# Gate and up products moved into the output projection's program, with their first two weight tiles loaded and split there

## The reference

```python
def finish_layer(x, o_n, o_f, g_n, g_f, w_o, g_post_mix, g_pre_ffn, g_post_ffn, w_gate, w_up, w_down):
    mixed = jnp.concatenate([rms_norm(o_n, g_n), rms_norm(o_f, g_f)], axis=-1) @ w_o
    x = x + rms_norm(mixed, g_post_mix)
    hf = rms_norm(x, g_pre_ffn)
    ffn = (jax.nn.silu(hf @ w_gate) * (hf @ w_up)) @ w_down
    return x + rms_norm(ffn, g_post_ffn)
```

## Time and profile before

| what | value |
|---|---|
| median of 3 runs | 1980.43 us (1977.78 to 1982.19) |
| the profiled execution | 1979.99 us, of it 1978.3 us span from first to last instruction |
| TensorE busy with matmuls | 1806.4 us, 91% of the span |
| VectorE, ScalarE, GpSimd busy | 917.3, 600.1, 266.2 us (46%, 30%, 13%) |
| mean granted clock of TensorE | 0.954 of full |
| gate and up products, three lines | 341.9 + 339.5 + 339.2 us busy, matmuls overlapping |

### The profile page before, as it was taken

How to read it: one execution, slowest core, us unless ns; L and a number is a source line. 1 busy time by engine, 2 the same in 40 slices (tenths; PEclk the granted TensorE clock), 3 DMA queues, 4 the chain that set the end, 5 groups by cost and what they waited for, 6 DMA issues and landing times. The chain is left out here.

```text
span 1978.3 us, 35180 instructions
## 1 busy us (share of the span) xinstructions
PE 1806.4 (91%) x13281; PEld 1603.1 (81%) x13281; DVE 917.3 (46%) x1845; ACT 600.1 (30%) x1206; POOL 266.2 (13%) x576
## 2 busy tenths in 40 slices
PE   7799998999875989899989969999999998999995
PEld 7799998777544767676658769999999998999995
DVE  4422422125524777777765533333333332655566
ACT  4100001223213656565665520011000001333334
POOL 3000024501431313232220000000000000000001
PEclk9999999999886999998989979999999999999997
DMA  5435956637997040302001221111111110111114
GB/s 146 156 90 148 227 145 119 217 107 244 341 271 159 2 97 2 80 19 86 2 33 64 88 56 42 53 42 48 47 42 42 53 43 21 44 43 38 42 48 186
DMA packets 158985, 184.64 MB, mean 93 GB/s; under 512 B 31207, under 2 KB 121690, under 8 KB 158802
## 3 DMA queue, kind: packets, MB, share of 16 engines
q1 hardware_dynamic: 132914, 137.47, 22.7%
q0 software_dynamic: 13088, 37.23, 7.1%
q10 hardware_dynamic: 12864, 8.39, 1.9%
HBM read 152.82 MB, written 34.38 MB: 95 GB/s over the span
## 5 line engine op out<-in xcount | busy, mean ns | idle before, releaser
L180 PE MATMUL psum<-hf_hi,gu_hi 128*128 128x352 f32 x1056 | 341.9, 324 | 9.0 <-DVE gu_lo L2610 9.0
L181 PE MATMUL psum<-hf_lo,gu_hi 128*128 128x352 f32 x1056 | 339.5, 321 | 0.0
L182 PE MATMUL psum<-hf_hi,gu_lo 128*128 128x352 f32 x1056 | 339.2, 321 | 0.0
L180 PEld LDWEIGHTS psum<-hf_hi,gu_hi 128*128 128x128 f32 x1056 | 199.1, 188 | 9.2 <-issue 9.2
L181 PEld LDWEIGHTS psum<-hf_lo,gu_hi 128*128 128x128 f32 x1056 | 199.3, 189 | 0.0
L182 PEld LDWEIGHTS psum<-hf_hi,gu_lo 128*128 128x128 f32 x1056 | 198.7, 188 | 0.0
L180 PE MATMUL psum<-h_hi,down_hi 128*128 128x352 f32 x528 | 174.1, 330 | 19.0 <-DVE h_lo L2709 19.0
L180 PE MATMUL psum<-x_hi,w_hi 128*128 128x352 f32 x528 | 172.9, 327 | 9.4 <-DVE w_lo L628 5.0
L1983 ACT ACTIVATE probs<-psum,neg_max 128x640 f32<-128x640 f32 (+7 forms) x192 | 138.2, 720 | 117.8 <-DVE neg_max L2126 114.3
L181 PE MATMUL psum<-h_lo,down_hi 128*128 128x352 f32 x528 | 172.5, 327 | 0.0
L182 PE MATMUL psum<-h_hi,down_lo 128*128 128x352 f32 x528 | 172.3, 326 | 0.0
(11 more groups left out here) (378 smaller groups left out, 3261.2 us busy)
## 6 DMA issues: line engine op xcount, KB each, us to landing
fox_ring<-in_cache_fox_kv SPq DMA_DIRECT2D x128, 256.0 KB, 6.1
zT<-z_stage SPq DMA_DIRECT2D x22, 528.0 KB, 2.9
w_ring<-in_w_in POOLq DMA_DIRECT2D x22, 512.0 KB, 5.3
gu_ring<-in_w_ffn_gate SPq DMA_DIRECT2D x22, 512.0 KB, 3.9
gu_ring<-in_w_ffn_up SPq DMA_DIRECT2D x22, 512.0 KB, 3.8
down_ring<-in_w_ffn_down SPq DMA_DIRECT2D x44, 256.0 KB, 2.7
nsa_page<-in_cache_nsa_kv POOLq DMA_DIRECT2D x64, 128.0 KB, 6.4
out<-nat SPq DMA_DIRECT2D x12, 512.0 KB
```

The source lines that it names most:

```text
L180: nc.tensor.matmul(dst, w_hi, x_hi, start=start, stop=False)
L181: nc.tensor.matmul(dst, w_hi, x_lo, start=False, stop=False)
L182: return nc.tensor.matmul(dst, w_lo, x_hi, start=False, stop=stop)
```

## The change

The gate and up products' block is taken out of build_e and its parts are appended to the five engines' lists in build_d's block. So one barrier falls away, and the first tile's products are written out ahead of the loop, in six groups of 24.

- Memory. `gate_up_tiles` lays gu_ring, gu_hi, gu_lo and silu where mixT (the projection's input) lies, and hT behind them, where build_d's own tiles lie. gu_ring may be written once mixT has been read for the last time ("m_lo" of tile 8), hT once all of x1 is stored.
- SyncE issues the first gate and up loads in turn t = QT - 1 = 7, ahead of that tile's store; the other 21 pairs in a loop behind the last store.
- VectorE splits both first tiles behind the low part of tile 6, ahead of tile 8's second sum. In the loop the gain is now multiplied in behind the wait for the products of the tile before.
- TensorE: gate blocks 0 and 1 behind the transposes of tile 7, up block 0, the transposes of tile 8, up block 1, gate block 2, up block 2, then a loop of 21 turns.
- ScalarE: silu of tile 0 behind its last step of build_d, then a loop of 21.

```diff
@@ -166,11 +166,13 @@
             w_o_loaded = sem("d_w_o_loaded")
             w_o = [low[name][:, 0, e, :] for name in ("q_fox", "k_fox", "decay") for e in range(2)]
             w_o += [low["v_fox"][:, 0].rearrange("p e t d -> p (e t d)"), k_slc[:, 0, :]]
+            with ExitStack() as first:
+                gate_up, hT = gate_up_tiles(nc, first)
             with ExitStack() as mixing:
                 mixT = sb(mixing, "mixT", [P, KD, N])
                 build_c(nc, a, o, c, env, mixT, low, w_o, w_o_loaded, squares)
-                build_d(nc, a, env, mixT, w_o, w_o_loaded, squares, hf_hi, hf_lo)
-            build_e(nc, a, env, hf_hi, hf_lo, ffn_out)
+                build_d(nc, a, env, mixT, w_o, w_o_loaded, squares, hf_hi, hf_lo, gate_up, hT)
+            build_e(nc, a, env, ffn_out, hT)
             build_f(nc, a, o, env, ffn_out)
 
 
@@ -2229,9 +2231,23 @@
     return names + [("turned", t, b) for t in (QT - 1, QT) for b in range(2)]
 
 
-def build_d(nc, a, env, mixT, w_o, w_o_loaded, squares, hf_hi, hf_lo):
-
-
+FG = 2
+
+
+def gate_up_tiles(nc, ctx):
+
+    def sb(name, shape, dt=F32):
+        return ctx.enter_context(nc.sbuf_tensor(name, shape, dt))
+
+    tiles = sb("gu_ring", [P, 2, KD, P]), sb("gu_hi", [P, 2, KD, P], F32R), sb("gu_lo", [P, 2, KD, P], F32R), sb("silu", [P, N])
+    sb("before_h", [P, 3 * 2 * FG * 2 * P + 4 * N - 3 * 2 * KD * P - N])
+    return tiles, sb("hT", [P, FT, N])
+
+
+def build_d(nc, a, env, mixT, w_o, w_o_loaded, squares, hf_hi, hf_lo, gate_up, hT):
+
+
+    gu_ring, gu_hi, gu_lo, silu = gate_up
     x1_dram, gains, psum, sem, ident, ones, eps = (env[k] for k in ("x1_dram", "gains", "psum", "sem", "ident", "ones", "eps"))
     ctx = ExitStack()
     with ctx:
@@ -2254,6 +2270,13 @@
         x_rstd = sb("d_x_rstd", [P, QT + 1])
         sampled = y[:, 0, 0:KD * S].rearrange("p (k n) -> p k n", k=KD)
         x_loaded, gain_loaded, x1_stored = [sem(f"d_x_loaded{s}") for s in range(2)], sem("d_gain_loaded"), sem("d_x1_stored")
+        gu_loaded = [sem("e_gate_loaded"), sem("e_up_loaded")]
+        gu_gained = [sem("e_gate_gained"), sem("e_up_gained")]
+        gu_high = [sem("e_gate_high"), sem("e_up_high")]
+        gu_split = [sem("e_gate_split"), sem("e_up_split")]
+        gu_done = [sem("e_gate_done"), sem("e_up_done")]
+        silu_ready, h_ready = sem("e_silu_ready"), sem("e_h_ready")
+        GU = [a[n][0].rearrange("(k p) n -> p k n", p=P) for n in ("w_ffn_gate", "w_ffn_up")]
         DA, DV, DP = Steps(sem("d_act"), d_act_order()), Steps(sem("d_dve"), d_dve_order()), Steps(sem("d_pe"), d_pe_order())
 
         def bank_of(t, h, g):
@@ -2277,12 +2300,20 @@
                 sp.dma_start(gain[:, :], a["norm_mix_post"].to_broadcast([P, D])).then_inc(gain_loaded, 16)
                 load(1)
                 for t in range(QT + 1):
+                    if t == QT - 1:
+                        for s in range(2):
+                            DV.wait(sp, ("m_lo", QT))
+                            sp.dma_start(gu_ring[:, s], GU[s][:, :, 0:P]).then_inc(gu_loaded[s], 16)
                     DV.wait(sp, ("added", t))
                     sp.dma_start(x1_dram[t * P:t * P + rows_of(t), :], x[0:rows_of(t), t % 2, :]).then_inc(x1_stored, 16)
                     if t + 2 <= QT:
                         sp.wait_ge(x1_stored, 16 * t + 16)
                         DA.wait(sp, ("hf", t))
                         load(t + 2)
+                with sp.Fori(0, FT - 1) as f:
+                    for s in range(2):
+                        sp.wait_ge(gu_split[s], f + 1)
+                        sp.dma_start(gu_ring[:, s], GU[s][:, :, bass.ds(f * P + P, P)]).then_inc(gu_loaded[s], 16)
                 sp.wait_ge(x1_stored, 16 * (QT + 1))
 
             @block.tensor
@@ -2326,8 +2357,32 @@
                         DP.done(step(t, h, range(KD)), ("done", t, h))
                         if h == 0 and t >= 2:
                             turn(t - 2)
+                def gate_up(s, b):
+                    for k in range(KD):
+                        tok = slice(b * NB, (b + 1) * NB)
+                        last = product(nc, psum[:, 3 * s + b, 0:NB], gu_hi[:, s, k, :], gu_lo[:, s, k, :], hf_hi[:, k, tok], hf_lo[:, k, tok], k == 0, k == KD - 1)
+                    return last
+
                 turn(QT - 1)
+                pe.wait_ge(gu_split[0], 1)
+                DV.wait(pe, ("lo", 5, 1))
+                gate_up(0, 0)
+                gate_up(0, 1)
+                pe.wait_ge(gu_split[1], 1)
+                DV.wait(pe, ("sum", QT, 1))
+                gate_up(1, 0)
                 turn(QT)
+                gate_up(1, 1)
+                DV.wait(pe, ("lo", QT, 1))
+                gate_up(0, 2).then_inc(gu_done[0], 1)
+                gate_up(1, 2).then_inc(gu_done[1], 1)
+                with pe.Fori(0, FT - 1) as f:
+                    for s in range(2):
+                        pe.wait_ge(gu_split[s], f + 2)
+                        pe.wait_ge((silu_ready, h_ready)[s], f + 1)
+                        for b in range(3):
+                            last = gate_up(s, b)
+                        last.then_inc(gu_done[s], 1)
 
             @block.scalar
             def _(act):
@@ -2391,6 +2446,18 @@
                     DA.done(nc.scalar.activation(y[0:n, t % 2, :], x[0:n, t % 2, :], ACT.Copy, scale=x_rstd[0:n, t:t + 1]), ("hf", t))
                 high(QT)
 
+                def silu_of(f):
+                    for b in range(3):
+                        last = nc.scalar.activation(silu[:, b * NB:(b + 1) * NB], psum[:, b, 0:NB], ACT.Silu)
+                    last.then_inc(silu_ready, 1)
+
+                act.wait_ge(gu_done[0], 1)
+                silu_of(0)
+                with act.Fori(0, FT - 1) as f:
+                    act.wait_ge(gu_done[0], f + 2)
+                    act.wait_ge(h_ready, f + 1)
+                    silu_of(f + 1)
+
             @block.vector
             def _(dve):
                 def m_low(t):
@@ -2414,6 +2481,22 @@
                         DA.wait(dve, ("hi", t, b))
                         tok = slice(t * P, t * P + n)
                         DV.done(nc.vector.tensor_tensor(hf_lo[:, 4 * b:4 * b + 4, tok], turned_in(t, b), hf_hi[:, 4 * b:4 * b + 4, tok].bitcast(F32), ALU.subtract), ("lo", t, b))
+
+                def split_weights(f, s):
+                    dve.wait_ge(gu_loaded[s], f * 16 + 16)
+                    nc.vector.tensor_tensor(gu_ring[:, s], gu_ring[:, s], gains[:, 2, :].unsqueeze(2).to_broadcast([P, KD, P]), ALU.mult).then_inc(gu_gained[s], 1)
+                    dve.wait_ge(gu_gained[s], f + 1)
+                    nc.vector.tensor_copy(gu_hi[:, s], gu_ring[:, s]).then_inc(gu_high[s], 1)
+                    dve.wait_ge(gu_high[s], f + 1)
+                    nc.vector.tensor_tensor(gu_lo[:, s], gu_ring[:, s], gu_hi[:, s].bitcast(F32), ALU.subtract).then_inc(gu_split[s], 1)
+
+                def gated(f):
+                    dve.wait_ge(gu_done[1], f + 1)
+                    dve.wait_ge(silu_ready, f + 1)
+                    dst = hT[:, f, :] if isinstance(f, int) else hT[:, bass.ds(f, 1), :].rearrange("p o n -> p (o n)")
+                    for b in range(3):
+                        last = nc.vector.tensor_tensor(dst[:, b * NB:(b + 1) * NB], psum[:, 3 + b, 0:NB], silu[:, b * NB:(b + 1) * NB], ALU.mult)
+                    last.then_inc(h_ready, 1)
 
                 m_low(0)
                 DV.done(nc.vector.memset(group[:, :, QT:QT + 1], 1.0), "cleared")
@@ -2453,8 +2536,18 @@
                     DV.done(nc.vector.reciprocal(x_rstd[0:n, t:t + 1], x_total[0:n, t:t + 1]), ("inverse_x", t))
                     if 0 < t < QT:
                         low(t - 1)
+                    if t == QT - 1:
+                        split_weights(0, 0)
+                        split_weights(0, 1)
                 low(QT)
-                DV.wait(dve, ("lo", QT, 1))
+                dve.wait_ge(x1_stored, 16 * (QT + 1))
+                with dve.Fori(0, FT - 1) as f:
+                    dve.wait_ge(gu_done[0], f + 1)
+                    split_weights(f + 1, 0)
+                    gated(f)
+                    split_weights(f + 1, 1)
+                gated(FT - 1)
+                dve.wait_ge(h_ready, FT)
 
 
 def build_f(nc, a, o, env, yT):
@@ -2540,96 +2633,15 @@
-def build_e(nc, a, env, hf_hi, hf_lo, yT):
+def build_e(nc, a, env, yT, hT):
...
-                            pe.wait_ge(split[s], f + 2)
-                            pe.wait_ge((silu_ready, h_ready)[s], f + 1)
...
-                        dve.wait_ge(loaded[s], f * 16 + 16)
-                        nc.vector.tensor_tensor(ring[:, s], ring[:, s], gains[:, 2, :].unsqueeze(2).to_broadcast([P, KD, P]), ALU.mult).then_inc(high[s], 1)
-                        dve.wait_ge(done[s], f + 1)
-                        dve.wait_ge(high[s], f * 2 + 1)
-                        nc.vector.tensor_copy(w_hi[:, s], ring[:, s]).then_inc(high[s], 1)
...
-            FG = 2
```

67 lines of the change are left out of this document (1 added, 66 removed).

## The result

The first four runs of the changed kernel have a median of 1958.17 us (1955.55 to 1959.13), beside 1979.95 us for the kernel before; the ratio is 0.9889 (95% interval 0.9876 to 0.9903). The profiled execution took 1958.33 us, its span is 1956.6 us. The forecast was 1961.2 us with a range from 1958.5 to 1966.5, so the direction was right and the time fell 0.3 us under the range. The difference, 21.2 us, is 2.4 us more than the 18.8 of the forecast. Where those 2.4 us come from is the question of the later experiments.

A forecast was written before the change was run, and what follows sets the result against it. TensorE was taken to bound the stretch except in two holes. Holes of 7.79 + 9.03 go, 0.85 comes, 2.70 of cold clock and 0.27 go, taken as 18.8: 1979.99 - 18.8 = 1961.2 us, range 1958.5 to 1966.5.

The forecast's parts named there:

- The loads: SyncE's two first weight loads, issued ahead of tile 7's store, cost nothing; cover over 5 us.
- The slide of tile 8's chain: Two splits on VectorE ahead of tile 8's second sum delay its chain of norms by 4.05 us.
- The slack of 0.1 us at the loop's first turn: Tile 1's split is ready at 1166.38 us, against TensorE wanting it at 1166.49.
- the price that was set on a cold one: Half clock at the program change cost 2.70 us in the first tile and 0.27 in tile 8's transposes.
- no run-ahead: Rival: gate products still wait for tile 8's chain, starting at 1155.9; only 3.9 us gained, 1976.1 us; chance 0.03.
- the loop's branch: Rival: TensorE's branch back fetches instructions each turn, 21 x 3.1 = 65 us, time 2026 us; chance 0.03.
- 1958.5 at the low end: Low end of the range, from earlier runs reaching 2.7 us below their median.
- What stands behind the products ... is not changed, so nothing gives it back: Down projection and end norms, behind the gate and up products, are unchanged, so the 18.8 us gain stays.
- The term for the end: From the last gating to the end of the span: no change forecast, 0 us.
- The stretch ahead of the seam: Everything before VectorE's low part of tile 6: no change forecast, 0 us.
- the seam: From VectorE's low part of tile 6 to its gating of tile 0; tile 1 begins 18.9 us earlier, taken as 18.8.

The follow-up runs named there:

- down_warm: Changed kernel plus 38 transposes into an unused bank at the start of the down projection's program, ahead of the semaphore count; median 1960.35 us, ratio 0.9896.
- down_warm2: Changed kernel plus 32 transposes at the start of the down projection's program, with the semaphore count given first; median 1956.47 us, ratio 0.9884.
- best: Changed kernel with earlier first gate load and split, down projection's first two weight tiles loaded ahead of the barrier, 17 transposes behind the semaphore count; median 1952.56 us.

## Why the prediction was right and where it fell short

Read from the start of tile 6's low part, its steps and what the first profile of the changed kernel shows:

| step | forecast | measured |
|---|---|---|
| first split begins | 1.22 | 1.21 |
| first gate product | 4.62 | 4.46 |
| scaled rows of tile 8 ready | 15.56 | 15.31 |
| tile 8's transposes begin | 16.07 | 16.12 |
| split of tile 1 begins | 24.78 | 24.76 |
| gating of tile 0 | 28.60 | 28.59 |

- The loads cost nothing, as forecast. The gate load was issued at 1125.97, the store that it passed went out at 1132.64.
- The slide of tile 8's chain was 4.05 in the forecast. Its sum came 1143.35 - 1135.90 = 7.45 us behind the low part and 3.65 us before, so 3.8 us. The forecast took 6.48 us for two splits from the earlier trace rows; here they took 1143.43 - 1137.11 = 6.32.
- The slack of 0.1 us at the loop's first turn held. The row of the page that groups the gate and up products (count, busy time, mean ns, idle time ahead of them) has 0.7 us of idle time, which is the first product's hole:

```profile
L182 PE MATMUL psum<-hf_hi,gu_hi 128*128 128x352 f32 x1056 | 340.8, 323 | 0.7 <-DVE gu_lo L2491 0.7
```

- The clock stayed up across the hole of 0.70 us, and the price that was set on a cold one, 2.70 and 0.27, was 2.95 when measured by itself (2.71 against the mean of five profiles).
- The two small rivals (no run-ahead, the loop's branch) didn't come: the turns take the same 22.89 us as before. The Trainium skill's rule on taken branches (Runtime: NRT & Kernel Launch, section Instruction fetch mechanics) had no effect at this loop at its new place.

Two steps failed, and with them the time lies under the range. **"1958.5 at the low end"** was taken from the spread of three runs, 1977.78 to 1982.19; ninety runs of the same kernel span 1975.42 to 1989.88, and a median of four has a share of that. **"What stands behind the products ... is not changed, so nothing gives it back"** put the end at nothing. The work there is unchanged, but its holes met the clock otherwise: none of them paid the 1.25 us of cold clock that one had paid before. The term for the end was 0 and measured 1.2. The stretch ahead of the seam was put at 0 too; it has the scatter. Of the 2.9 us by which the changed kernel's first profile lies under 1961.2, 2.3 lie ahead of the seam and 0.5 in the end, so that the first four runs fell below the range is in part luck: the median of all thirteen, 1959.13, lies inside. The mechanism and the size of the seam were right to 0.1 us.

## What to carry to other kernels

A hole between two programs is three costs at once (the barrier, the first load, and half clock behind it), and what closes it is independent work that the waiting engine can run in it: moving the preparation alone gave less than a third here, 5.8 of 18.9 us. When a stretch moves, the holes behind it meet the clock otherwise, so a microsecond may come or go in work that was not edited: look at when the clock fell, ahead of the hole's end or behind it. Take the spread of a forecast from many runs, and measure a change by a stretch inside the profile that both kernels have.

## What the runs showed of the hardware

- The same hole of 3.84 us on TensorE cost 1.3 us more or not, by how long the clock had been at half when it ended (0.60 us or more in the twelve that paid, 0.57 or less in the 48 that didn't). The five profiles of the kernel before paid in the same quarter, and the three of the changed kernel in none; the other kernels were profiled once each.
- Running transposes did not by itself hold the clock: behind a hole of 1.96 us they ran at 0.59 in down_warm, though TensorE was busy for 3.00 of 3.00 us, and behind 2.11 us at 0.50 in down_warm2. Behind 2.11 us in best they ran at 1.00. What decides between the two was not found.
- A hole of 0.70 us ahead of the first gate product left the clock at 1.00.
